# TensorE's programs for both MLPs written out for all eight chunks, in place of one turn, an engine loop of six, and one turn

## The reference

```
a = relu(rms_norm(h) @ w1)          # w1: 2048 x 8192
h = h + (a * a) @ w2                # w2: 8192 x 2048
```

## Time and profile before

| | |
|---|---|
| time, median of 3 runs | 2160.84 us (2160.17 to 2161.29) |
| span of the profiled execution | 2160.0 us |
| PE (TensorE matmuls) busy | 2019.7 us, 94% |
| PEld (TensorE weight loads) busy | 1987.4 us, 92% |
| DVE (VectorE) busy | 1244.9 us, 58% |
| ACT (ScalarE) busy | 885.8 us, 41% |
| DMA traffic | 338.66 MB, mean 157 GB/s |

### The profile page before, as it was taken

One profiled execution on the slowest core, in us unless ns is written; L12 is line 12 of the kernel. 1 busy time (PEld: TensorE's weight loads), 2 busy tenths in 40 slices (PEclk: granted clock), 3 DMA queues, 4 the chain that ended last, 5 costly groups with the idle time before them and its releaser, 6 DMA issues.

```text
span 2160.0 us, 39380 instructions
## 1 busy us (share of the span) xinstructions
PE 2019.7 (94%) x16332; PEld 1987.4 (92%) x16332; DVE 1244.9 (58%) x1268; ACT 885.8 (41%) x1047; POOL 155.9 (7%) x91
## 2 busy tenths in 40 slices
PE   6575797999999999999999999999999999999998
PEld 5475797999999999999999888999999999999998
DVE  6989773544545454545476666665555555555554
ACT  4251353343424343434355445554434444344443
POOL 2837300000000000000000011000000000000000
PEclk9797898999999999999999999999999999999999
DMA  6211157555555555555554423556565655656564
GB/s 183 61 43 30 57 177 169 175 174 159 176 152 175 153 175 157 176 153 175 176 170 148 142 89 113 171 167 198 187 187 185 181 189 185 186 185 184 185 185 137
DMA packets 188846, 338.66 MB, mean 157 GB/s; under 512 B 23112, under 2 KB 27416, under 8 KB 188376
## 3 DMA queue, kind: packets, MB, share of 16 engines
q1 hardware_dynamic: 171200, 331.52, 49.4%
q10 hardware_dynamic: 17384, 4.77, 1.4%
q0 software_dynamic: 128, 0.34, 0.1%
HBM read 334.11 MB, written 2.14 MB: 156 GB/s over the span
## 4 chain that ended last, share of the span: by engine, by line
PE 85%; DVE 11%; issue 2%; ACT 1%; ACTq 1%; DMA 0%; SPq 0%; DVEq 0%
PE acc L257 80%; DVE wlo L241 2%; DVE z L1311 1%; ACTq L927 1%; PE acc L717 1%; DVE tb L1328 1%; PE acc L721 1%; DVE hg_lo L289 1%; PE acc L690 0%; DMA ms<-in_meta_tokens 0%; DVE rot L1302 0%; DVE z L1305 0%; PE acc L588 0%; DVE rot L1308 0%; PE acc L704 0%
## 5 line engine op out<-in xcount | busy, mean ns | idle before, releaser
L241 DVE TENSOR_TENSOR wlo<-raw,whi 128x1024 fp32r<-128x1024 f32 x624 | 767.8, 1235 | 712.9 <-ACT whi L236 712.7
L236 ACT ACTIVATE whi<-raw 128x1024 fp32r<-128x1024 f32 x624 | 658.8, 1058 | 1086.4 <-PE acc L257 1066.7
L257 PE MATMUL acc<-hg_hi,whi 128*128 128x256 f32 (+1 forms) x2496 | 722.7, 290 | 54.4 <-DVE wlo L241 38.7
L257 PE MATMUL acc<-hg_hi,wlo 128*128 128x256 f32 (+1 forms) x2496 | 718.7, 288 | 11.1 <-issue 11.1
L257 PE MATMUL acc<-hg_lo,whi 128*128 128x256 f32 (+1 forms) x2496 | 716.2, 287 | 0.0
L257 PE MATMUL acc<-a_hi,whi 128*128 128x272 f32 (+1 forms) x2176 | 619.0, 284 | 1.5 <-DVE a_lo L1374 1.5
L257 PE MATMUL acc<-a_hi,wlo 128*128 128x272 f32 (+1 forms) x2176 | 617.9, 284 | 0.0
L257 PE MATMUL acc<-a_lo,whi 128*128 128x272 f32 (+1 forms) x2176 | 616.4, 283 | 0.0
L257 PEld LDWEIGHTS acc<-hg_hi,whi 128*128 128x128 f32 x2496 | 479.3, 192 | 72.4 <-issue 42.4
L257 PEld LDWEIGHTS acc<-hg_lo,whi 128*128 128x128 f32 x2496 | 477.4, 191 | 0.1
L257 PEld LDWEIGHTS acc<-hg_hi,wlo 128*128 128x128 f32 x2496 | 477.3, 191 | 0.0
(11 more groups left out here) (235 smaller groups left out, 1283.9 us busy)
## 6 DMA issues: line engine op xcount, KB each, us to landing
raw<-in_mlp_w SPq DMA_DIRECT2D x512, 512.0 KB, 3.8
raw<-in_attn_w_qkv SPq DMA_DIRECT2D x40, 512.0 KB, 3.7
raw<-in_attn_w_o SPq DMA_DIRECT2D x32, 512.0 KB, 4.0
raw<-in_s_w_in SPq DMA_DIRECT2D x16, 512.0 KB, 4.1
raw<-in_s_w_out SPq DMA_DIRECT2D x16, 512.0 KB, 4.8
raw<-in_s_w_glu SPq DMA_DIRECT2D x8, 512.0 KB, 3.8
xs<-in_x SPq DMA_DIRECT2D x2, 1024.0 KB, 7.5
bias_w<-bias_by_distance ACTq DMA_DIRECT2D x2, 1024.0 KB, 13.7
```

Source lines behind the costliest of these rows:

```text
L236: nc.scalar.activation(whi[:, k, :, :], raw[:, k, :, :], ACT.Copy).then_inc(sem("hi_split"), 1)
L241: nc.vector.tensor_tensor(wlo[:, k, :, :], raw[:, k, :, :], whi[:, k, :, :], ALU.subtract).then_inc(sem("lo_split"), 1)
L257: m = nc.tensor.matmul(o, w[:, k, t, 128 * n:128 * n + 128], xx[:, kt + t, cols], start=first and t == 0 and j == 0 and not (packed and n ...
```

## The change

TensorE's program for each MLP is written out chunk by chunk. The loop, its register and the register forms of the counts go; the waits compare with constants. The order of matmuls, waits and signals is the same, and no other engine's program is touched: ScalarE, VectorE and SyncE keep their loops.

```diff
-        def mlp_pe(pe, H, G, layer, c, i, cols):
-            def c_val(base, per):
-                return base + per * c if i is None else base + per * i
-            h0, g0 = (H + 32 * c, G + 6 * c) if i is None else (H, G)
+        def mlp_pe(pe, H, G, layer, c, cols):
+            h0, g0 = H + 32 * c, G + 6 * c
...
-                mm_group(pe, h0 + 8 * g, i, g0 + g, i, *gained[k], 8, cols, ready)
+                mm_group(pe, h0 + 8 * g, None, g0 + g, None, *gained[k], 8, cols, ready)
...
-                        pe.wait_ge(sem("a_ready"), c_val(16 * layer + j // 2 + 1, 2))
-                mm_group(pe, h0 + 16 + 4 * g, i, g0 + 2 + g, i, a_hi, a_lo, 4, atok, ready)
+                        pe.wait_ge(sem("a_ready"), 16 * layer + 2 * c + j // 2 + 1)
+                mm_group(pe, h0 + 16 + 4 * g, None, g0 + 2 + g, None, a_hi, a_lo, 4, atok, ready)
...
-            mlp_pe(pe, H_MLP0, G_MLP0, 0, 0, None, ALLT)
-            with pe.Fori(1, 7) as c:
-                mlp_pe(pe, H_MLP0, G_MLP0, 0, None, c, ALLT)
-            mlp_pe(pe, H_MLP0, G_MLP0, 0, 7, None, ALLT)
+            for c in range(8):
+                mlp_pe(pe, H_MLP0, G_MLP0, 0, c, ALLT)
...
-            mlp_pe(pe, H_MLP1, G_MLP1, 1, 0, None, REAL)
-            with pe.Fori(1, 7) as c:
-                mlp_pe(pe, H_MLP1, G_MLP1, 1, None, c, REAL)
-            mlp_pe(pe, H_MLP1, G_MLP1, 1, 7, None, REAL)
+            for c in range(8):
+                mlp_pe(pe, H_MLP1, G_MLP1, 1, c, REAL)
```

More of the change, by code:

```diff
@@ L349, in ready @@
                 def ready(j):
-                    if i is None and c == 0 and g == 0 and j % 2 == 0:
+                    if c == 0 and g == 0 and j % 2 == 0:
                         pe.wait_ge(sem("hg_ready"), 4 * k + j // 2 + 1)
-                    if i is None and c == 0 and g == 0 and j == 6:
+                    if c == 0 and g == 0 and j == 6:
                         pe.wait_ge(sem("group_out"), g0)
                         norm_pe(pe, k, STAT_BANK[k], cols)
-                if i is None and c == 0 and g == 1:
+                if c == 0 and g == 1:
                     pe.wait_ge(sem("var_ready"), k + 1)
-                mm_group(pe, h0 + 8 * g, i, g0 + g, i, *gained[k], 8, cols, ready)
+                mm_group(pe, h0 + 8 * g, None, g0 + g, None, *gained[k], 8, cols, ready)
             for g in range(4):
```

## The result

The changed kernel takes 2126.89 us (median of 4 runs, 2124.44 to 2128.88), the kernel before 2160.51 us (2159.52 to 2161.29). The ratio is 0.9841, with a 95% interval of 0.9829 to 0.9853: 33.6 us less. The forecast was 2126.6 us.

A forecast was written before the change was run, and what follows sets the result against it. TensorE was taken to bound the kernel, carrying 85% of the chain of waits. Removing MLP 0's jumps gave 2160.84 - 34.27 = 2126.6 us, every other term 0; the range was 2124.3 to 2130.5 us.

The forecast's parts named there:

- The five jumps of MLP 0: TensorE, MLP 0 chunks 2 to 6: standstill and lower clock behind each jump back go, saving 34.27 us.
- MLP 1 and the registers: TensorE: removing MLP 1's five jumps (0.01 us at most each) and turning registers into constants in 12 passes gains nothing.
- The added program: Instruction DMA: ten repeated passes become new code, 30 more packets in MLP 1; taken as 0, bounds 0 and 53 us.
- the near row: MLP 1's chunk 1, which loads 6 packets beside the data stream without loss: the ground for the 0 bound.
- Other engines' jumps without cover: MLP 0: ScalarE, VectorE and SyncE now jump beside running matmuls; nothing, at worst 5.57 us per chunk.
- Code behind the loops: Later code shifts against instruction blocks; the attention stage's 1.5 us wait may go or get a sister: taken as 0.
- They lie differently against the blocks: Equally long TensorE loop bodies: block placement makes MLP 0's reload each turn while MLP 1's stays; no separate size.
- the rival's 2092 us: MLP 1's five jumps hide the same loss, 6.85 us each, so the time would be 2092.3 us; chance 1%.
- The term in the MLPs: TensorE's busy time in MLP 0's chunks 2 to 6, expected to fall by 11.7 us.
- The range of its own: Whole kernel: 2125.1 to 2128.1 us around the forecast, from the shift of the code; forecast case 93%.

The follow-up runs named there:

- e1: Kernel before, with ScalarE, VectorE and SyncE written out in both MLPs and TensorE keeping its loops: 2159.96 us, ratio 0.9996.
- e4: Kernel before, with only MLP 0 of TensorE's program written out and MLP 1 keeping its loop: 2125.92 us, ratio 0.9841.
- e2: Kernel before, both TensorE loops kept, each body's first instruction moved to place 64 of a 256-instruction block: 2127.22 us, ratio 0.9851.
- e8: Changed kernel, with ScalarE, VectorE and SyncE written out as well, so no engine jumps: 2125.82 us, ratio 0.9844 to the kernel before.
- e3: Kernel before, both TensorE loop bodies moved to begin at place 230 of a 256-instruction block: 2182.61 us, ratio 1.0099.
- e5: Kernel before, TensorE loops kept, MLP 0's body moved to begin at place 208 and MLP 1's at 220: 2150.70 us, ratio 0.9955.
- e6: Kernel before, TensorE loops kept, each body given a hint at its top naming the closing branch and its target: 2126.56 us, ratio 0.9847.
- e9: Kernel before, both TensorE loop bodies moved to place 230 and given the hint on the closing branch: 2127.97 us, ratio 0.9844.
- e7: Kernel before, TensorE loop bodies made two chunks long, so two jumps in each MLP instead of five: 2148.80 us, ratio 0.9945.
- e10: Kernel before, TensorE loop bodies made two chunks long and given the hint on the closing branch: 2123.13 us, ratio 0.9827.

## Why the prediction was right

**The five jumps of MLP 0.** Forecast 34.27 us. Chunks 2 to 6 took 515.32 us and now take 481.07, so the trace gives 34.25; the medians differ by 33.6 us. The standstill and the lower clock behind it went together. That the standstill is TensorE's own was argued from the code; e1 and e4 show it. That it waits for its program can also be read in the kernel before: each of the two stops at the first jump (526.5 to 529.27 us and 529.27 to 531.94) holds one packet of the instruction queue.

```profile
q8 instruction: 1, 0.02, 2.2%
```
```profile
q8 instruction: 1, 0.02, 2.1%
```

**MLP 1 and the registers.** Forecast nothing, measured nothing: e4 without this half has the same time, and e2 keeps the registers in both MLPs at no cost.

**The added program.** Forecast nothing for about 30 packets in MLP 1. They came (30) and its chunks stay at 90.69 us. Of the bounds, 0 and 53 us, the near row was right. The count was 129 or a few more, and 128 came.

**Other engines' jumps without cover.** Forecast nothing; e8 takes them away and gains nothing.

**Code behind the loops.** Taken as 0, with 1.5 us either way. The wait of 1.5 us in the attention stage is there as before:

```profile
PE acc L257 <- issue: 1.5, 1, 1.5
```

**Why MLP 0 pays and MLP 1 doesn't.** "They lie differently against the blocks" was a guess from two rows. e2, e3 and e5 turn it into a result: the time follows the place, either way, for either MLP. The rule of the Trainium skill that was weighed there ("Runtime: NRT & Kernel Launch", Instruction fetch mechanics: a jump beyond a two-page window waits for its page) would have both loops pay, and would have given the rival's 2092 us. On TensorE a jump back over 1578 instructions costs nothing in e2, e6 and e9. Its other half, that a jump to a page that isn't there waits for it, agrees with the traces, at 3.7 to 7.9 us for one jump.

**What was off.** PE's busy time was to fall by 11.7 us and fell by 8.4. The term in the MLPs was right (chunks 2 to 6 are at 96.2 busy of 96.2), but I let all else stand, and this execution has 281.3 us of it against 279.2 in the attention stage, and 224.7 against 223.7 in the stage ahead of MLP 0: my test went by the whole page where only the stretch counts. And place 231, which I counted for MLP 0's head in what I expected of e2 and e7, is wrong. From place 230 there are 26 instructions left in the block, and 12 matmuls ran before the second stop, 24 of them with the loads; in the kernel before 5 matmuls and 6 loads ran, so there were some 13 left and the head lay near 243. Nothing in the forecast hung on it. In e7 a jump of MLP 1 cost 4.8 and 4.6 us in place of 2.5 to 4: TensorE stood still for 3.2 and 2.9 us, and the sum had left out the lower clock behind that.

The range of its own (2125.1 to 2128.1) held the median, but single runs of the changed kernel reach from 2124.4 to 2128.9, so that the median came within 0.3 us of the forecast is in part luck. What lies outside the loops moves by itself: chunk 0 of MLP 0 takes 110.4 to 112.8 us over the kernels here, and the attention stage 284.2 to 285.9. The span profiled after the change is 2127.1 us against the 2125.7 of the sum, with 0.9 of the 1.4 us in the attention stage.

## What to carry to other kernels

Before writing out a loop, cut the trace at its passes and compare the first with the rest: a loop whose passes behind the jump are as long as its first has nothing to give, however long its body, and its twin elsewhere may lose 7 us a turn. The instruction queue says why in one line: packets in a pass that repeats mean a body that doesn't stay. Whether that costs time, only the lengths say: in e10 the packets come and cost nothing. Here writing out, moving the head within its block, or a hint on the closing branch gave the same 33 to 34 us; the place alone is fragile, since any instruction added ahead of the loop moves it, and the hint also serves bodies that can't fit.

## What the runs showed of the hardware

- Packets of the instruction queue are of 16 KB (2.10 MB / 128), and a written-out chunk of 1543 instructions brings 6. The second stop fits blocks of 256 too: from place 230 12 matmuls run ahead of it (e3), from 220 17 (e5), which with their loads and 2 more instructions are the 26 and 36 that are left of 256. The limit of e5 lies between 1786 and 1798 instructions from the start of the first block, which fits seven such blocks.
- Seven blocks of a TensorE loop stay without the hint, eight with it (e9), and thirteen do in neither form (e7, e10). The reading that fits all of these is that eight are held and that the one loaded ahead at the end of the body takes the head's room. That load is in the trace of e3 and not in that of e9; the packets show that blocks are loaded, not which are thrown out, so that last part is inferred.
- In straight code and in e10, 6 or 7 packets per chunk arrive beside a data stream of 175 to 186 GB/s without a stop.
- A miss costs more than the loads: 2.0 to 3.2 us to the first matmul, a second stop when the head's block is short, and then in most cases matmuls at the 1.2 GHz level (granted share 0.50 in stretches of e3, 0.64 over one of the earlier trace rows) after the engine had stood still. At the last jump of MLP 1 in e3 and in e5 the granted clock stayed at 1.00, and they cost 5.0 and 3.7 us.
- Setting the head's place can have a price of its own, once: the loop's first pass takes 0.8 and 1.0 us more in MLP 0 at place 230 (e3, e9) and 0.5 us in MLP 1 at 220 (e5). It takes nothing more in MLP 1 at 230, in MLP 0 at 208, or at 64; why, no run shows.
